# Turning the gated product in 32x32 squares on VectorE, with 16 small transfers per block

## The reference, cut to what matters

```python
def swiglu(x, w_gate, w_up, w_down):
    return (jax.nn.silu(x @ w_gate) * (x @ w_up)) @ w_down

h = h + 0.5 * swiglu(rms_norm(h, norm), w_gate, w_up, w_down)    # four times
h = h + 0.5 * swiglu_2(rmsnorm(h, norm), w_in, w_out)            # four times, gate and up in one matrix
```

## Time and profile before

| | |
|---|---|
| median of 3 runs | 1971.68 us (1971.55 to 1972.51) |
| profiled execution | 1972.77 us, its span 1971.0 us |
| TensorE busy | 1960.5 us (99%) |
| VectorE busy | 1199.4 us (61%) |
| ScalarE busy | 1018.6 us (52%) |
| granted TensorE clock | 1.00 |
| transfers | 338.91 MB, mean 172 GB/s |

### The profile page before, as it was taken

How to read it: one execution, slowest core, us unless ns; L and a number is a source line. 1 busy time by engine, 2 the same in 40 slices (tenths; PEclk the granted TensorE clock), 3 DMA queues, 4 the chain that set the end, 5 groups by cost and what they waited for, 6 DMA issues and landing times.

```text
span 1971.0 us, 26229 instructions
## 1 busy us (share of the span) xinstructions
PE 1960.5 (99%) x9838; PEld 1652.8 (84%) x9838; DVE 1199.4 (61%) x1817; ACT 1018.6 (52%) x1590; POOL 68.9 (3%) x77
## 2 busy tenths in 40 slices
PE   9999999999999999999999999999999999999999
PEld 7888988888888898888888898888888888888887
DVE  6555656556655566555755566655576555876554
ACT  6444555445554665444544447544475444755442
POOL 0100300000000000000000000000010000200000
PEclk9999999999999999999999999999999999999999
DMA  9655436553655426555555434555446553306550
GB/s 339 210 202 174 150 108 214 192 191 130 221 184 178 144 77 212 192 192 171 188 181 186 162 138 139 203 192 192 171 163 234 183 189 128 108 24 212 192 192 22
DMA packets 241050, 338.91 MB, mean 172 GB/s; under 512 B 5728, under 2 KB 206351, under 8 KB 240831
## 3 DMA queue, kind: packets, MB, share of 16 engines
q1 hardware_dynamic: 239710, 335.84, 50.5%
q0 software_dynamic: 496, 1.23, 0.2%
q10 hardware_dynamic: 752, 0.61, 0.1%
HBM read 336.61 MB, written 1.05 MB: 171 GB/s over the span
## 4 chain that ended last, share of the span: by engine, by line
PE 95%; DVE 2%; ACT 2%; DMA 1%; issue 0%; SPq 0%; POOL 0%; ACTq 0%
PE A L535 11%; PE A L537 11%; PE A L536 11%; PE G L535 10%; PE G L537 10%; PE G L536 10%; PE X L535 8%; PE X L537 8%; PE X L536 8%; PE A L1226 1%; PE A L904 1%; PE G L964 1%; PE X L964 1%; PE X L1210 1%; PE G L1238 1%; DVE wl L496 0%
## 5 line engine op out<-in xcount | busy, mean ns | idle before, releaser
L496 DVE TENSOR_TENSOR wl<-raw,wh 128x1024 fp32r<-128x1024 f32 (+1 forms) x553 | 653.8, 1221 | 121.3 <-ACT wh L487 120.3
L487 ACT ACTIVATE wh<-raw 128x1024 fp32r<-128x1024 f32 (+1 forms) x553 | 561.9, 1058 | 144.1 <-PE A L537 102.6
L535 PE MATMUL G<-wh,xh 128*128 128x512 f32 (+1 forms) x814 | 322.1, 396 | 0.2
L537 PE MATMUL G<-wh,xl 128*128 128x512 f32 (+1 forms) x814 | 317.2, 390 | 0.0
L536 PE MATMUL G<-wl,xh 128*128 128x512 f32 (+1 forms) x814 | 316.3, 389 | 0.0
L535 PE MATMUL X<-wh,xh 128*128 128x512 f32 x672 | 265.8, 395 | 0.3 <-DVE wl L496 0.3
L537 PE MATMUL X<-wh,xl 128*128 128x512 f32 x672 | 262.3, 390 | 0.0
L536 PE MATMUL X<-wl,xh 128*128 128x512 f32 x672 | 261.6, 389 | 0.0
L537 PEld LDWEIGHTS G<-wh,xl 128*128 128x128 f32 x814 | 152.8, 188 | 32.3
L535 PEld LDWEIGHTS G<-wh,xh 128*128 128x128 f32 x814 | 152.9, 188 | 30.9 <-DVE xl L2399 0.6
L536 PEld LDWEIGHTS G<-wl,xh 128*128 128x128 f32 x814 | 153.1, 188 | 29.9
(11 more groups left out here) (487 smaller groups left out, 2787.5 us busy)
## 6 DMA issues: line engine op xcount, KB each, us to landing
raw<-in_ffn_w_in SPq DMA_DIRECT2D x88, 1024.0 KB, 6.8
raw<-in_ffn_w_down SPq DMA_DIRECT2D x44, 1024.0 KB, 6.5
raw<-in_ffn_w_out SPq DMA_DIRECT2D x44, 1024.0 KB, 7.1
raw<-in_ffn_w_gate SPq DMA_DIRECT2D x42, 1024.0 KB, 5.5
raw<-in_ffn_w_up SPq DMA_DIRECT2D x42, 1024.0 KB, 7.5
raw<-in_a_w_in SPq DMA_DIRECT2D x12, 1024.0 KB, 6.1
raw<-in_ab_w_in SPq DMA_DIRECT2D x8, 1024.0 KB, 6.8
raw<-in_kv_w SPq DMA_DIRECT2D x6, 1024.0 KB, 6.5
```

What stands on the lines that cost most here:

```text
L487: nc.scalar.activation(hi, r, ACT.Copy).then_inc(hi_done[u], 1)
L496: nc.vector.tensor_tensor(lo, r, hi.bitcast(F32), ALU.subtract).then_inc(lo_done[u], 1)
L535: nc.tensor.matmul(o, sh, rh, start=start, stop=False)
L537: return nc.tensor.matmul(o, sl, rh, start=False, stop=stop)
```

## The change

In blocks 0 to 9 of each layer TensorE turns nothing. VectorE transposes `hid` in 32x32 squares in one instruction over 512 columns (`turn_squares`), each square inside its own band of 32 partitions. That leaves square (g, q) in the wrong band, so ScalarE's queue issues 16 transfers from SBUF to SBUF, 32 partitions by 128 float32 (16 KB) each, that put the squares in place (`move_squares`). The high and low parts are then read from `squares_out` in SBUF. The last block of each layer is still turned by TensorE. Silu is taken in one pass, so that `hidden` has one instruction per token tile and not two, and `rstd2` goes.

```diff
                 def step(b, turn=None):              # TensorE
                     gate_up(b, 0, turn)
-                    turn_hid(b - 1, turn)
                     gate_up(b, 1, turn)
                     down(b - 1, turn)
...
                     for t in range(NT):              # ScalarE, sigmoid(b)
-                        A_(sig[:, t, :], GB[b % 2][t][:, 0:S], ACT.Sigmoid, scale=rstd[:, t:t + 1]).then_inc(sig_ready, 1)
+                        A_(sig[:, t, :], GB[b % 2][t][:, 0:S], ACT.Silu, scale=rstd[:, t:t + 1]).then_inc(sig_ready, 1)
+
+                def move_squares(b, turn=None):
+                    at = 0 if turn is None else 2 * turn
+                    act.wait_ge(squares_turned, (FFN_BLOCKS - 1) * f + b + 1 + at)
+                    for g in range(4):
+                        for q in range(4):
+                            act.dma_start(squares_out[32 * g:32 * (g + 1), q, :],
+                                          squares_in[32 * q:32 * (q + 1), g, :]).then_inc(squares_moved, 16)
 
                 def hid_hi(b, turn=None):
-                    at = 0 if turn is None else 4 * turn
+                    at = 0 if turn is None else 512 * turn
+                    act.wait_ge(squares_moved, 256 * ((FFN_BLOCKS - 1) * f + b + 1) + at)
                     for t in range(NT):
-                        act.wait_ge(hid_turned, 2 * (FFN_BLOCKS * f + b) + t + 1 + at)
+                        A_(hid_view(hidh, b, t), moved_view(t), ACT.Copy).then_inc(hidh_done, 1)
...
                     for u in (0, 1):                 # ScalarE, step(b)
                         if (1, u) not in split:
                             prepare_hi(base + 2 * b + 1, u, turn)
+                    move_squares(b - 1, turn)
                     for half in (0, 1):
                         prepare_hi(base + 2 * b + half, 2, turn)
                     hid_hi(b - 1, turn)
...
                     for t in range(NT):              # VectorE, hidden(b)
                         dve.wait_ge(sig_ready, n + t + 1)
-                        V.tensor_tensor(gated[:, t, :], GB[b % 2][t][:, 0:S], sig[:, t, :], ALU.mult).then_inc(gated_done, 1)
-                    for t in range(NT):
-                        dve.wait_ge(gated_done, n + t + 1)
-                        V.scalar_tensor_tensor(hid[:, t, :], GB[b % 2][t][:, S:2 * S], rstd2[:, t:t + 1], gated[:, t, :],
+                        V.scalar_tensor_tensor(hid[:, t, :], GB[b % 2][t][:, S:2 * S], rstd[:, t:t + 1], sig[:, t, :],
                                                ALU.mult, ALU.mult).then_inc(hid_done, 1)
+
+                def turn_squares(b, turn=None):
+                    at = 0 if turn is None else 4 * turn
+                    dve.wait_ge(hid_done, 2 * (FFN_BLOCKS * f + b) + 2 + at)
+                    V.transpose(squares_in.rearrange("p g (c t j) -> p t c g j", c=2, t=NT),
+                                hid.rearrange("p t (c g j) -> p t c g j", c=2, g=4)).then_inc(squares_turned, 1)
...
                     hidden(b - 1, turn)              # VectorE, step(b)
+                    turn_squares(b - 1, turn)
```

More of the change, by code:

```diff
@@ L354, in blocks_program @@
         sig = cut(work, 0, 2, S)
-        gated, hid = cut(work, 2 * S, 2, S), cut(work, 4 * S, 2, S)
+        hid = cut(work, 2 * S, 2, S)
+        squares_in, squares_out = cut(work, 4 * S, 4, P), cut(work, 6 * S, 4, P)
         PT = cut(work, 0, 2, TRI)
@@ L375, in blocks_program @@
         xhi_done, xlo_done, acc_done = sem("xhi_done"), sem("xlo_done"), sem("acc_done")
-        sig_ready, gated_done, hid_done = sem("sig_ready"), sem("gated_done"), sem("hid_done")
+        sig_ready, hid_done = sem("sig_ready"), sem("hid_done")
+        squares_turned, squares_moved = sem("squares_turned"), sem("squares_moved")
         hid_turned, hidh_done, hidl_done = sem("hid_turned"), sem("hidh_done"), sem("hidl_done")
@@ L537, in mm3, with moved_view, hid_view @@
             return nc.tensor.matmul(o, sl, rh, start=False, stop=stop)
+        def moved_view(t):
+            return squares_out.rearrange("p b (c t j) -> p c b t j", c=2, t=NT)[:, :, :, t, :]
+        def hid_view(x, b, t):
+            return x[:, b % 2, t * S:(t + 1) * S].rearrange("p (c b j) -> p c b j", c=2, b=4)
         ML_T = ((A[2], A[3]), (G[0], G[1]))
@@ L956, in gate_up, with turn_hid @@
                     last.then_inc(used[1], 1)
-                def turn_hid(b, turn=None):
-                    at = 0 if turn is None else 4 * turn
+                def turn_hid(b):
                     for t in range(NT):
-                        pe.wait_ge(hid_done, 2 * (FFN_BLOCKS * f + b) + t + 1 + at)
+                        pe.wait_ge(hid_done, 2 * (FFN_BLOCKS * f + b) + t + 1)
                         for j in range(2):
@@ L1017, in ffn @@
                 gate_up(end, 0)
-                turn_hid(end - 1)
                 gate_up(end, 1)
@@ L1793, in sigmoid, with last_hid_hi @@
                     for t in range(NT):
-                        A_(sig[:, t, :], GB[b % 2][t][:, 0:S], ACT.Sigmoid, scale=rstd[:, t:t + 1]).then_inc(sig_ready, 1)
+                        A_(sig[:, t, :], GB[b % 2][t][:, 0:S], ACT.Silu, scale=rstd[:, t:t + 1]).then_inc(sig_ready, 1)
[6 more added lines that the diff above has]
+                                          squares_in[32 * q:32 * (q + 1), g, :]).then_inc(squares_moved, 16)
                 def hid_hi(b, turn=None):
-                    at = 0 if turn is None else 4 * turn
+                    at = 0 if turn is None else 512 * turn
+                    act.wait_ge(squares_moved, 256 * ((FFN_BLOCKS - 1) * f + b + 1) + at)
                     for t in range(NT):
-                        act.wait_ge(hid_turned, 2 * (FFN_BLOCKS * f + b) + t + 1 + at)
+                        A_(hid_view(hidh, b, t), moved_view(t), ACT.Copy).then_inc(hidh_done, 1)
+                def last_hid_hi():
+                    b = FFN_BLOCKS - 1
+                    for t in range(NT):
+                        act.wait_ge(hid_turned, 2 * f + t + 1)
                         A_(hidh[:, b % 2, t * S:(t + 1) * S], GB[b % 2][t][:, 0:S], ACT.Copy).then_inc(hidh_done, 1)
@@ L1861, in ffn @@
                     prep(name, FT + 1, (0, 1))
-                hid_hi(FFN_BLOCKS - 1)
+                last_hid_hi()
             def start(name):
@@ L1910, in _ @@
             act.wait_ge(dve_chain, 1)
-            A_(zinv[:, 0:1], y[:, 0, 0:1], ACT.Sigmoid)
+            A_(zinv[:, 0:1], y[:, 0, 0:1], ACT.Silu)
             def small_weights():
@@ L1961, in fox_mixer @@
                     last = A_(decay[at:at + FOX_H, :], A[3][at:at + FOX_H, 0:S], ACT.Copy, scale=-1.0)
-                last.then_inc(event("fox_sums_hi"), 1)
+                last.then_inc(event("gate_hi"), 1)
                 wait_half(act, "fox", *ROWS["fox"][1][:2])
@@ L2072, in mlstm_mixer @@
                     last = A_(decay[at:at + ML_H, :], mls["top"][at:at + ML_H, 0, P:], ACT.Copy, scale=-1.0)
-                last.then_inc(event("ml_top_hi"), 1)
+                last.then_inc(event("gate_hi"), 1)
                 def gates(chunks):
@@ L2460, in hid_lo, with last_hid_lo @@
                         dve.wait_ge(hidh_done, 2 * (FFN_BLOCKS * f + b) + t + 1 + at)
+                        V.tensor_tensor(hid_view(hidl, b, t), moved_view(t), hid_view(hidh, b, t).bitcast(F32),
+                                        ALU.subtract).then_inc(hidl_done, 1)
+                def last_hid_lo():
+                    b = FFN_BLOCKS - 1
+                    for t in range(NT):
+                        dve.wait_ge(hidh_done, 2 * (FFN_BLOCKS * f + b) + t + 1)
                         part = slice(t * S, (t + 1) * S)
@@ L2527, in ffn @@
                     prep(name, FT + 1, (0, 1))
-                hid_lo(FFN_BLOCKS - 1)
+                last_hid_lo()
                 if name == "ffn0":
@@ L2650, in fox_mixer @@
                 split_keys(1)
-                dve.wait_ge(event("fox_ln"), 1)
+                dve.wait_ge(event("gate_ln"), 1)
                 V.scalar_tensor_tensor(fox["logf"], fox["z"], 0.0, fox["e"], ALU.min, ALU.subtract
```

13 lines of the change are left out of this document (6 added, 7 removed).

## The result

The changed kernel takes 2158.17 us, median of 4 runs (2154.5 to 2159.91), against 1972.1 us for the kernel before (4 runs, 1971.55 to 1973.58). The ratio is 1.094, with a 95% interval of 1.0923 to 1.0957. The forecast was 1956.5 us with a range of 1938 to 1982. It is wrong in sign.

The account below looks back on a forecast made before the run. TensorE, busy 99% of the span, was taken as the bound: 36.8 us of transposes removed, less first-step waits of 10.5, 5.1, 3.5 and 2.5, gives -15.2 us and 1956.5 us, range 1938 to 1982.

Parts of the forecast that it names:

- the steady step: Blocks 1 to 9 of each layer: ScalarE's round of 13.85 us stays under TensorE's 16.34, so 72 steps are hidden.
- c: Distance from issue to issue of the 16 transfers on ScalarE's queue: 0.42 us, between 0.35 and 0.47.
- L: Time from the last issue's start to its landing: 2.3 us, 3.0 in ffn0; rows from 2.0 to 3.4.
- Silu to first issue: On ScalarE, Silu's start to the end of the two copies behind it: 2.62 us, VectorE ready at 2.1.
- last issue's start to `hid_hi`: On ScalarE, the landing of 2.3 us and a hop of 0.06, with the two down weight copies hidden under it.
- `hid_hi` to the next Silu: On ScalarE, from the start of `hid_hi` to the end of the next two copies: 2.57 us.
- 15c + L = 11.1: Point past which ScalarE's round exceeds TensorE's 16.34 us; from about 10.6 the layers' first steps already eat the whole gain.
- The first steps: Each layer's first `down` waits on `hidl`: 10.5 us over six layers, 5.1 in ffn0, 3.5 in ffn4, 2.5 more in ffn2.
- Rival A: ScalarE's queue becomes the bound through 16 issues ahead of `hid_hi` and the next Silu: 2003 us, chance 0.19.
- B: Nearly the whole gain: early issues and quick landings, only ffn0 and ffn4 stand still, some 3 us: 1938 us, chance 0.10.
- C: Gain all spent in layers' first steps, issue distance and landing both at their upper rows: 1972 us, no change, chance 0.07.
- D: Silu's table has no Copy, so two table loads of 1.28 us stand in each ScalarE round: 1972 us or slower, chance 0.04.

Follow-up runs that it names:

- from_hbm_on_act: Changed kernel, its 16 transfers still on ScalarE's queue but reading x in HBM instead of the squares in SBUF (product wrong): 2061.53 us.
- turn_first: Changed kernel with VectorE's products and transpose put ahead of the low parts of the block's weights from step(2) on: 2154.83 us, ratio 1.0927.
- no_transfers: Changed kernel with the 16 transfers left out, parts read from VectorE's squares in the wrong bands: 1934.96 us.
- eight_on_act: Changed kernel with 8 of the 16 transfers left out, so half of the squares are not moved: 1977.83 us.
- eight_held: Changed kernel with only 8 transfers on ScalarE's queue, SyncE holding the next weight loads until they land, by a needless 8 KB store: 1949.9 us.
- by_hbm_early: Changed kernel with SyncE moving squares through HBM, one transfer out and four back; ffn0's block 0 goes out before the third down load: 1941.98 us, ratio 0.9844.
- eight_and_eight: Changed kernel with 8 transfers issued by SyncE and 8 by ScalarE, nothing left out: 1958.0 us, ratio 0.9921.

## Why the prediction was wrong

**The step that failed is the sum of the steady step**, ScalarE's round of 5.25 + 15c + L = 13.85 us. It is 18.28, over TensorE's 16.34. The terms:

| term | forecast | measured | us a round |
|---|---|---|---|
| 15c | c 0.42 | c 0.641 | +3.32 |
| Silu to first issue | 2.62 | 3.55 | +0.93 |
| last issue's start to `hid_hi` | 2.36 | 2.60 | +0.24 |
| `hid_hi` to the next Silu | 2.57 | 2.51 | -0.06 |

The largest miss is c. With the measured c and all else as forecast, the round is 5.25 + 9.62 + 2.3 = 17.2 and already over. I had bounded c by 0.35 to 0.47 from the earlier trace rows. They agree with transfers out of HBM in this kernel too (0.473 in *from_hbm_on_act*), but the change copies SBUF to SBUF. The prediction said that no row shows this and still took its ends from rows of the other kind. The row nearest to the truth was GpSimd's 0.54, kept for a rival. The trace before also has an issue of SyncE behind which the next starts only 0.52 us later (kv_norm, at 143.82), outside the range. A term multiplied by 15 in every round deserved an upper end beyond the nearest rows: the decision point 15c + L = 11.1 is c = 0.59 at the L taken, not far above 0.47.

A better c would not have saved the forecast. *from_hbm_on_act* has c at 0.473 and its round is 17.29 us, since two other terms were taken too small: the first issue comes at 3.10 instead of 2.62, and the last issue's start to `hid_hi` is 4.31 instead of 2.36. By these rows the round reaches TensorE's 16.34 at (16.34 - 3.10 - 4.31 - 2.53) / 15 = 0.43, an estimate, which lies inside the range for c. The 2.3 taken for L is right in the kernel after only because its issues are so slow that the loads are nearly in; with faster issues the last square lands beside them. The prediction had a row of 3.4 for that and used it for the end of the range alone.

The second term is a slack that was counted once and then vanished. In the earlier trace rows ScalarE waits for TensorE ahead of the sigmoid, and in the earlier trace rows VectorE, its low parts done, waits for the sigmoid; once ScalarE and VectorE are the bound, nobody waits there, and VectorE's two low parts for the next block stand in front of the products. *turn_first* shows that taking this off buys nothing, since the landing moves into its place.

In the third term the two down copies lie under L as forecast, but they last until 945.77, longer than the landing (2.3 us from the last issue's start). So here the copies set `hid_hi`, and not L. It costs little.

**The first steps.** Forecast 21.6 us in sum. From Silu to Silu the eight measured periods are 138.9 us against 82.8 in *no_transfers*: 56. The place was right (TensorE's first `down` on `hidl`). The size was wrong by the same c and by a term of VectorE's: from the start of `hid_hi` to the end of `hidl` the forecast has 1.18 us, and ffn1 shows 2.21 (347.13 to 349.34), for the low parts of the down weights (346.31 to 348.67) now stand ahead of it. Where the issues are few, it is a landing of 5.7 us beside the loads in place of 2.3, as *eight_on_act* and *eight_held* show.

**The account.** From *no_transfers* to the kernel after are 223 us: 72 x (18.28 - 16.32) = 141 in the regular rounds, 56 in first steps. The other some 26 are 4 behind the last blocks and, for the rest, steady rounds longer than 18.28. ScalarE's rows say which part of these is long: the issues by some 15 us in sum, with single ones of up to 2.07, the time from the last issue to `hid_hi` by 7, and ffn2's piece of work behind `step(2)` by 5. TensorE's stretches at half clock can hardly be the reason, since Silu doesn't wait for TensorE in these rounds.

**Rival A** named the mechanism, the place and the point from which it decides. Its price was 31 us over before and is 186, since it was worked out with c at 0.56 and the first issue at 2.62: a round of 16.65 us against 18.28. Its chance was 0.19, and both follow from the same narrow bound. B's time, 1938, is what the change gives if the moves are hidden (1935 to 1942). C needed both at their upper rows, and c lies above them; *from_hbm_on_act*, with c just there, takes 2061.5 us and not C's 1972. D is false: five table loads stand at L1802, none between Silu and copies in the steady round, and the loads of ffn2 in the earlier trace rows are gone.

**What was right.** The transposes have left TensorE but for the last blocks' (first row below; L964 before), and *no_transfers* gives 37.5 us for the forecast 36.8. Silu in one pass is worth nothing. VectorE's transpose takes 0.71 us, forecast 0.75 (second row):

```profile
L974 PE MATMUL G<-const,work 128*128 128x128 f32 x32 | 4.8, 272 | 0.0
```
```profile
L2482 DVE STREAM_TRANSPOSE work<-work x80: 711/712/715, 26.1 to 2128.1; 128x512 f32<-128x512 f32 x80
```

## What to carry to other kernels

An issue of a transfer is an instruction of its engine: count it per issue, by the memories that it goes from and to, and give a price that is multiplied by many an upper end beyond rows of another kind. The last landing of a batch has two prices, with the big loads beside it and without, and making the issues faster can turn one into the other. Before using slack, write down the round of the engine that is to spend it and how far it is from the bound; past that point the slack of its neighbours goes too. Few wide transfers, even with a detour through HBM, beat many narrow ones: what was lost was issuing, not bytes.

## What the runs showed of the hardware

- An issue from SBUF to SBUF takes 0.61 us on ScalarE and 0.59 on SyncE, with 32 rows or with 128; from HBM to SBUF 0.44 on ScalarE (*from_hbm_on_act*) and 0.43 on SyncE, from SBUF to HBM 0.35 on SyncE (*by_hbm_early*).
- Two queues issuing at once hardly slow each other: 0.61 us an issue on ScalarE and 0.59 on SyncE (medians of *eight_and_eight*), as alone.
- Issues start while earlier instructions of the same engine still run: in ffn1 at 334.98, when the two copies from 333.55 end at 335.55.
- A transfer of 16 KB lands in 1.8 us (median) when no big load is about, in 5.2 beside loads of 1 MB.
- After TensorE stood for 5.83 us it ran at 1.2 GHz until 353.47, about 4 us; after the pause of 1.60 us at 929.66 it stayed at 2.4 GHz, and after the one of 1.90 us at 404.93 it was at 1.2.
